# Attention masks of a two-mixer encoder step: from identity products on TensorE to in-place additions on VectorE

## The reference, cut to what matters

```python
# mixer A: a window of 128 keys back in chunks of 64, with a learned sink logit per head
s = einsum(q, k) * 0.125 ;  s = where(mask, s, -inf)
m = maximum(max(s), sink) ; e = exp(s - m) ; p = e / (sum(e) + exp(sink - m)) ; o = p @ v
# mixer B ("fox"): a forget term and a causal mask
s = einsum(q, k) * 0.125 + F[t] - F[s] ;  s = where(pos_k <= pos_q, s, -inf)
o = softmax(s) @ v
```

## Time and profile before

| | |
|---|---|
| time, median of 3 runs | 2954.06 us (2953.28 to 2956.42) |
| the profiled execution | 2956.46 us, of which the span from the first to the last instruction is 2954.9 us |
| PE busy | 2835.8 us (96%) |
| DVE busy | 1244.1 us (42%) |
| ACT busy | 856.9 us (29%) |
| POOL busy | 120.6 us (4%) |
| mean granted TensorE clock | 0.983 of full speed |

### The profile page before, as it was taken

One profiled execution on the slowest core, in us unless ns is written; L12 is line 12 of the kernel. 1 busy time (PEld: TensorE's weight loads), 2 busy tenths in 40 slices (PEclk: granted clock), 3 DMA queues, 4 the chain that ended last, 5 costly groups with the idle time before them and its releaser, 6 DMA issues.

```text
span 2954.9 us, 51431 instructions
## 1 busy us (share of the span) xinstructions
PE 2835.8 (96%) x21021; PEld 2760.4 (93%) x21021; DVE 1244.1 (42%) x1759; ACT 856.9 (29%) x1377; POOL 120.6 (4%) x190
## 2 busy tenths in 40 slices
PE   7799999999899889999999999999999999998998
PEld 6688899999899889999999999999999999997998
DVE  7544443434634373333333333333333333355732
ACT  4344343434522162212222221222122112213511
POOL 0200121111100000000000000000000000000000
PEclk8899999999999999999999999999999999999999
DMA  4110122222122122222222222222222222222231
GB/s 166 46 36 29 59 85 79 74 73 81 62 65 77 64 80 79 86 80 86 86 76 82 86 86 86 86 73 86 87 79 86 79 86 81 83 74 63 87 110 52
DMA packets 65270, 230.72 MB, mean 78 GB/s; under 512 B 9280, under 2 KB 10176, under 8 KB 64576
## 3 DMA queue, kind: packets, MB, share of 16 engines
q1 hardware_dynamic: 57312, 211.31, 22.2%
q0 software_dynamic: 6160, 15.41, 1.6%
q10 hardware_dynamic: 1616, 1.18, 0.1%
HBM read 217.71 MB, written 10.16 MB: 77 GB/s over the span
## 4 chain that ended last, share of the span: by engine, by line
PE 92%; DVE 3%; issue 2%; ACT 2%; DMA 1%; ACTq 0%; DVEq 0%; POOL 0%; POOLq 0%
PE tile L354 81%; PE misc L519 3%; PE misc L354 3%; PE misc L499 1%; PE misc L463 1%; PE misc L462 1%; ACT w_hi L705 1%; DMA sv<-in_swa_cv 1%; DVE stat L1107 0%; PE misc L441 0%; PE tile L553 0%; PE misc L502 0%; PE misc L467 0%; DVE st L1041 0%; DVE acc L1035 0%
## 5 line engine op out<-in xcount | busy, mean ns | idle before, releaser
L354 PE MATMUL tile<-x_hi,w_hi 128*128 128x288 f32 (+1 forms) x4000 | 882.4, 302 | 37.5 <-DVE x_lo L1098 12.7
L354 PE MATMUL tile<-x_hi,w_lo 128*128 128x288 f32 (+1 forms) x4000 | 856.9, 296 | 0.0
L354 PE MATMUL tile<-x_lo,w_hi 128*128 128x288 f32 (+1 forms) x4000 | 856.6, 296 | 0.0
L354 PEld LDWEIGHTS tile<-x_hi,w_hi 128*128 128x128 f32 (+1 forms) x4000 | 640.3, 189 | 66.2 <-issue 54.8
L354 PEld LDWEIGHTS tile<-x_lo,w_hi 128*128 128x128 f32 (+1 forms) x4000 | 643.8, 189 | 1.2
L354 PEld LDWEIGHTS tile<-x_hi,w_lo 128*128 128x128 f32 (+1 forms) x4000 | 643.6, 189 | 1.3
L705 ACT ACTIVATE w_hi<-w_raw 128x1024 fp32r<-128x1024 f32 x394 | 406.3, 1052 | 637.5 <-PE tile L354 618.0
L1025 DVE TENSOR_TENSOR w_lo<-w_raw,w_hi 128x1024 fp32r<-128x1024 f32 x394 | 474.7, 1222 | 214.7 <-ACT w_hi L705 214.6
L354 PE MATMUL tile<-hid_hi,w_hi 128*128 128x288 f32 x2048 | 437.2, 295 | 7.9 <-DVE acc L1321 7.9
L354 PE MATMUL tile<-hid_lo,w_hi 128*128 128x288 f32 x2048 | 437.4, 294 | 0.0
L354 PE MATMUL tile<-hid_hi,w_lo 128*128 128x288 f32 x2048 | 434.5, 293 | 0.0
(11 more groups left out here) (216 smaller groups left out, 1956.5 us busy)
## 6 DMA issues: line engine op xcount, KB each, us to landing
w_raw<-in_w SPq DMA_DIRECT2D x394, 512.0 KB, 3.6
acc<-in_x SPq DMA_DIRECT2D x4, 1152.0 KB, 9.5
out_y<-st POOLq DMA_DIRECT2D x16, 288.0 KB, 2.6
out_fox_v<-v_t POOLq DMA_DIRECT2D x8, 288.0 KB, 2.4
out_fox_k<-k_t POOLq DMA_DIRECT2D x8, 288.0 KB, 2.4
c_t<-in_ck POOLq DMA_DIRECT2D x8, 256.0 KB, 3.0
c_v<-in_cv POOLq DMA_DIRECT2D x8, 256.0 KB, 2.9
p_raw<-in_p POOLq DMA_DIRECT2D x1, 576.0 KB, 4.0
```

The lines of the kernel that those rows point to most:

```text
L354: ins = nc.tensor.matmul(dst[:, h, :], w, x[:, h * HALF:(h + 1) * HALF], start=first and a == 0, stop=last and a == 2)
```

## The change

The third product goes from `score`, in every call. DVE adds the mask to the same columns, in place in the score bank, ahead of the row maximum, and waits for that addition before it takes the maximum. In the loops the chain's counts grow by 16 (swa, 8 masked steps in each of two pairs) and by 20 (fox, 10 in each of two). The masks stay in the tensors `win_r` and `tri_r`, read as plain float32. The sink column (L480) isn't in the masked range.

```diff
-                    def score(at, width, ka, kb, key, mask=None):
+                    def score(at, width, ka, kb, key):
...
-                        last = nc.tensor.matmul(dst, qb[:, head, lhs], kb[:, head, key:key + width], start=False,
-                                                stop=mask is None)
-                        if mask is not None:
-                            m, mw = mask
-                            last = nc.tensor.matmul(scores_ps[:, at + width - mw:at + width], ident_r[:, :], m,
-                                                    start=False, stop=True)
-                        return last
+                        return nc.tensor.matmul(dst, qb[:, head, lhs], kb[:, head, key:key + width], start=False, stop=True)
...
                     at, width = span(kind, j)
+                    qt = step_of(j)[1]
+                    if kind == "swa" and qt < 4:
+                        end, mask = at + width - 1, win_r[:, 128:256] if qt == 0 else win_r[:, :]
+                    elif kind == "fox":
+                        end, mask = at + width, tri_r[:, 0:128] if qt < 4 else tri_r[:, 64:128]
+                    if kind == "fox" or qt < 4:
+                        tail = scores_ps[:, end - mask.shape[1]:end]
+                        chain.add(V.tensor_tensor(tail, tail, mask.bitcast(f32), ALU.add))
+                        chain.wait()
                     V.reduce_max(stat[:, j % 3, 0:1], scores_ps[:, at:at + width], AX, negate=True).then_inc(negmax, 1)
...
-                chain.enter(i, 2 * STEPS)
+                chain.enter(i, 2 * STEPS + 16)
...
-                chain.enter(i, 2 * STEPS)
+                chain.enter(i, 4 * STEPS)
```

More of the change, by code:

```diff
@@ L472, in attend @@
                         if qt == 0:
-                            score(at, 128, k1, k2, 0, (win_r[:, 128:256], 128))
+                            score(at, 128, k1, k2, 0)
                         elif qt < 4:
-                            score(at, 256, k1, k2, 128 * (qt - 1), (win_r[:, :], 256))
+                            score(at, 256, k1, k2, 128 * (qt - 1))
                         else:
@@ L483, in attend @@
                         if qt < 4:
-                            ins = score(at, 128 * (qt + 1), k1, k2, 0, (tri_r[:, :], 128))
+                            ins = score(at, 128 * (qt + 1), k1, k2, 0)
                         else:
                             score(0, PAST, fc1, fc2, 0)
-                            ins = score(512, SAMPLE, k1, k2, PROMPT, (tri_r[:, 64:128], SAMPLE))
+                            ins = score(512, SAMPLE, k1, k2, PROMPT)
                     ins.then_inc(scored, 1)
```

## The result

The changed kernel takes 2968.58 us (median of 5 runs, 2968.30 to 2970.18) against 2954.07 us (5 runs, 2953.28 to 2958.26) of the kernel before: a ratio of 1.0047, interval 1.0032 to 1.0062, or 14.5 us slower. The forecast was 2957.6 us. The time lies just inside the range, and the sign is that of the rival with the falling clock.

The account below looks back on a forecast made before the run. PE, busy 92% of the span, was taken as the bound, with attention latency-bound once per swa pair. Terms +5.5 + 0.8 - 5.6 + 2.8 = +3.5 us gave 2957.6 us against the median of 2954.06; range 2946 to 2969.

Parts of the forecast that it names:

- the rival with the falling clock: Swa pairs: longer PE waits drop the clock to 1.2 GHz; four of seven pairs cost +6.4 us, 2964; chance 0.20.
- The price of the addition: DVE, each masked step: 0.42 us for 256 columns, 0.29 for 128, 0.22 for 64.
- The rival of a dearer addition in PSUM: Swa links and slots: at 0.60 us for 256 columns, 9.7 us more, 2967; chance 0.20.
- The walk of the swa pair: Swa pair: three additions ahead of slot 4's transpose, less PE's savings, net +0.79 us; seven pairs +5.5.
- The hiding rival: Swa: additions hide, so swa gains 7.5 us rather than losing 6.3; time 2943.8; chance 0.15.
- a granted clock of 0.5 behind these waits: Swa pairs: half clock behind PE's waits, named as a sign that the prediction is wrong.
- The rule that was cited: Skill's rule that waiting each iteration can pay the clock transition each time; all seven swa pairs would pay, 2969.
- The first swa pair: Same walk, with additions up to the long 3.4 us wait and one behind slot 7: taken as +0.8 us.
- Seven fox pairs: Additions hide under weight steps, so PE's savings count whole: 7 x 0.80 = -5.6 us.
- the product's price: Fox mask product, read as distance to the next start: 0.11 us behind a 128-column score, 0.06 behind a wider.
- no pair would begin to stand for `f_pt`: Fox: PE starting to wait for `f_pt` outside the last pair would show the prediction wrong.
- The last fox pair: ACT and DVE chain up to score 9: additions lie on it whole, PE's savings are worth nothing; +2.8 us.

Follow-up runs that it names:

- experiment 3: Changed kernel plus 12 zero-adding products in PE's wait ahead of score 4 of each swa pair: 2959.02 us, ratio 1.0018 to the kernel before.
- experiment 7: Changed kernel (all masks on DVE) with the weight unit moved from c = 8 to c = 5: 2935.28 us, ratio 0.9941 to the kernel before.
- experiment 4: Changed kernel with the additions removed too, so no masks on either engine: 2947.81 us, ratio 0.9985 to the kernel before.
- experiment 2: Changed kernel with swa masks back as products on PE, only fox masks on DVE: 2949.76 us, ratio 0.9989 to the kernel before.
- 5: Changed kernel with additions only in fox pairs 0 to 6; swa and last fox pair keep PE products: 2946.64 us, ratio 0.9979 to the kernel before.
- 10: The kernel before once more, unchanged, one execution: 2950.87 us.
- 8: Changed kernel with the weight unit at c = 5 and the last fox pair's masks back on PE: 2933.35 us, ratio 0.9935 to the kernel before.
- run 9: The changed kernel once more, unchanged, one execution: 2970.43 us.
- run 11: Changed kernel with swa masks back on PE, only fox masks on DVE, once more, one execution: 2946.46 us.
- 6: Kernel before (all masks on PE) with the weight unit moved from c = 8 to c = 5: 2943.73 us, ratio 0.9975.
- experiment 1: Changed kernel with fox masks back as products on PE, only swa masks on DVE: 2972.22 us, ratio 1.0072 to the kernel before.

## Why the forecast was right in its parts and wrong in its case

**The price of the addition** was right: 0.429, 0.297 (fox; 0.293 in swa) and 0.229 us (the sample's) against 0.42, 0.29 and 0.22. The rival of a dearer addition in PSUM falls. By the table of the Trainium skill (VectorE: DVE Perf Modes, the section on the TRN2 errata) 256 columns would be 0.39 us; the trace has 0.429, so the table is too low here, as the rows of before already said of the maximum.

**The walk of the swa pair** was right: +0.79 us forecast, +0.84 measured where the clock holds (experiment 3). Over seven pairs that is 5.9 us, where 5.5 stood in the sum. The hiding rival falls for this order of the work, since no swa period got shorter, and comes true once the unit is moved (experiment 7).

**What failed is the choice between forecast and clock rival.** "The gaps are short, and a pair where it falls shifts the next" was the argument against the clock, with a chance of 0.20, and the rival was priced at four pairs of 1.6 us. It fell in all seven, for 1.4 us or 2.4 us each (2.9 in the last): the prediction had itself named a granted clock of 0.5 behind these waits as a sign that it is wrong. The swa pairs 2 to 8 together are 16.5 + 3.75 = 20.3 us longer; less 5.9 of latency, 14.4 us are the clock's, 2.1 per pair. The runs agree from the other side: experiment 3 gives back 9.6 us, with one fall of 1.4 left and 3.4 of stops come back, 14.4 together. The shift that was to save the next pair saved none; at most it decided between a short and a long fall, which no run tested. The rows for a better chance were there. In the earlier trace rows PE's share of the stretch was 2.41 of 3.3 us with no fall and 1.67 of 3.4 with one. The prediction itself forecast waits of 1.7 and 1.0 us in such a stretch; 3.3 - 2.7 leaves some 0.6 us of work, well below the 1.67 that fell (1.55 were measured, over a stretch cut a little differently). The rule that was cited (the Trainium skill, TensorE: Matmul & The Clock Gate, "HAM oscillation"), that a kernel with a wait in each iteration can pay the transition each time, gave seven pairs and 2969 us. The page's own example waits longer for its transfers than PE waits here, so the prediction stretched it. Of the kernel after that is what the trace shows; of the kernel before, with its shorter waits in each pair, and of pair 2 in experiment 4 it is not. That 2969 also met the total (2968.6) is partly luck, since it held 1.6 us per fall and knew nothing of the stops.

**The first swa pair:** +0.8 forecast, +0.2 measured (48.15 to 48.25 us with the masks on PE in runs before, 2, 5 and 10, and 48.3 to 48.7 with them on DVE in the old order). How much of the three additions its long wait of 3.4 us took in was not tested by itself.

**Seven fox pairs:** 0.80 us each was forecast, and 0.95 came (experiment 2, outside the stops); over seven pairs 1.1 us more. The term that was mis-sized is the product's price. The prediction read it as the distance to the next start: 0.06 us behind a wide score and 0.11 behind a narrow one. One place of PE's timeline, before:
```profile
448.00 0.22 PE L467 MATMUL misc<-tri_r,ident_r 128*128 128x128 f32 x1
448.06 0.48 PE L354 MATMUL tile<-x_hi,w_hi 128*128 128x288 f32 x2
448.38 0.42 PE L354 MATMUL tile<-x_lo,w_hi 128*128 128x288 f32 x2
```
and the same place after:
```profile
467.21 0.42 PE L354 MATMUL tile<-x_hi,w_hi 128*128 128x288 f32 x2
467.47 0.43 PE L354 MATMUL tile<-x_lo,w_hi 128*128 128x288 f32 x2
```
The first two weight products take 0.32 us behind a mask and 0.26 without. So the mask costs some 0.12 where weight products follow, half of it behind the next start, and the distance to the next start isn't the whole price. That no pair would begin to stand for `f_pt` was right: PE has no wait at all between 384 and 780 us. The other 3.2 us in fox are the two stops that vanished. No step of the prediction foresaw them. It said that PE stands for nothing in seven fox pairs, where the same view of the earlier trace rows has 2.7 us of "issue", the two stops.

**The last fox pair:** +2.8 forecast, +2.75 measured from score 0 to PE's restart (38.93 to 41.68 us). Experiments 2, 5, 7 and 8 show that the additions lie on the chain there, but put them at 3.5 to 3.6 us, and run 9, the kernel after again, restarts after 43.43 us, 4.5 later. What differs is the clock. Stretches of the kernel after in this pair:
```profile
811.10:814.50 3.40, 1.02 (x6) 0.72 (x7) 2.94 (x7) 2.21 (x7) 0.00 (x0) 1.00 0.00 0
814.50:817.90 3.40, 3.08 (x14) 2.78 (x12) 2.57 (x7) 1.57 (x5) 0.00 (x0) 0.50 0.08 8
```
A fall some 11 us behind score 0 is in every kernel without mask products on PE in this pair, and in none with them. Where it lasts 3.4 us (the kernel after, run 9, experiment 3), score 9 comes 29.6 to 30.0 us behind score 0; where it lasts 6.8 (experiments 2 and 7, run 11), 30.4 to 30.5. With no masks and a fall of 3.4 us it is 27.3, against 26.7 before. By these differences the additions are worth 2.3 to 2.7 us and a fall 0.6 to 1.4 (an estimate), and run 9 has a second fall at 834.9, ahead of the restart. The prediction saw the clock rival in swa only; that 2.8 met 2.75 is partly luck.

**The sum, put right:** 3.5 forecast, + 14.4 clock, + 0.4 walk, - 0.6 first pair, - 3.2 stops, - 1.3 for the fox products (pair 7 with them), + 0.4 outside the table: 13.6, against 13.5 between the spans. The last pair needs no term in this one execution.

**What stays open:** why the stops of 1.2 to 1.8 us at two turns of the fox loop are in some kernels only. They are in the kernels before, 2, 3, 5 and 6 and not in the kernel after, 1, 4, 7 and 8, wherever the masks are, and they repeat in each. The transfers of the instruction queue go with them. Between 505 and 690 us every kernel with stops has this line, and no kernel without stops has any:
```profile
q8 instruction: 13, 0.21, 0.5%
```
So the stops belong to kernels whose fox loop has its instructions transferred again in each turn. That this is what PE waits for is likely and not shown, and no run tested what decides it; kernel 1 and the kernel before have the same PE code in fox, so the place of the code is a guess. In all kernels PE also stands 9.9 us at some 144 us, in the first swa pair, again by "issue"; it is in both and takes no part in the difference.

## What to carry to other kernels

Ahead of moving work off an engine that others wait for, walk one iteration and ask what fills the engine's time in its wait: a product that looks like pure cost can be part of what keeps TensorE at 2.4 GHz, and a wait lengthened by a quarter of a microsecond can cost more than the work saved (experiment 4). Where the stretch around a wait will be emptier than one in the same trace behind which the clock fell, a fall in every iteration deserves more than one chance in five. And where a chain becomes too long, look at the longest link and not at the new one: moving a weight unit of 2.3 us by three steps turned a loss of 14.5 us into a gain of 18 (the vanished stops are in both numbers). The price of a product is read from what follows it as well as from the next start.

## What was unexpected of the hardware

- The clock fell though PE had work and its longest wait was 0.81 us (experiment 4, pairs 3 to 8: 2.34 us busy in a stretch of 3.6, clock 0.50 behind it), and didn't behind the same waits in pair 2, nor with 2.41 in 3.3.
- Products that add nothing, put in the wait, made the kernel 9.6 us faster (experiment 3). Moving the unit was worth more.
- At half clock PE's busy time hides the loss: it read 2835.8 us before and 2836.2 after with 144 matmuls fewer. The granted clock of the stretch, 1.00 against 0.90 to 0.95 over a swa pair, is the number that tells.
- An addition in place in PSUM costs the same as a maximum over it (0.429 for 256 columns and 0.425 us for 257).
- A loop whose PE code is unchanged lost two stops of 1.4 and 1.8 us when code elsewhere changed (experiment 1), and its instruction transfers with them. With effects of 3 us in question, such stops have to be subtracted pair by pair, ahead of any reading of the total.
